# Up projections of twelve tile pairs a layer as Strassen block products, interleaved with the down projection of the chunk before

## The reference, cut to what matters

```python
for l in range(2):
    mod = (silu(c) @ w_ada[l] + b_ada[l])[:, None, :]          # 6 x 1024
    sh1, sc1, g1, sh2, sc2, g2 = jnp.split(mod, 6, axis=-1)
    ...                                                         # mixers
    x = x + g1 * (concat(y_conv, y_ret) @ w_out[l])
    h2 = rms_norm(x, norm2_g[l]) * (1.0 + sc2) + sh2
    x = x + g2 * (jnp.square(jax.nn.relu(h2 @ w_up[l])) @ w_down[l])
return rms_norm(x, final_g)
```

## Time and profile before

| | |
|---|---|
| median of 3 runs | 1188.54 us (1188.49 to 1188.67) |
| the profiled execution | 1189.33 us |
| its span, first to last instruction | 1187.5 us |
| mean granted TensorE clock | 0.989 of full |
| w_raw loads | 200 of 512 KB, median 3.3 us to landing |
| ada loads | 80 of 512 KB, median 4.7 us to landing |

### The profile page before, as it was taken

The page is one execution under the profiler, slowest core; times in us unless marked ns, Lnnn a source line. Parts: engine busy times, 40 slices in busy tenths (PEclk is TensorE's granted clock), DMA queues, the critical chain, the costliest instruction groups (busy, mean ns, idle before and its releaser), DMA issues.

```text
span 1187.5 us, 17267 instructions
## 1 busy us (share of the span) xinstructions
PE 1154.9 (97%) x5690; PEld 974.5 (82%) x5690; DVE 656.8 (55%) x870; ACT 440.6 (37%) x623; POOL 252.4 (21%) x193
## 2 busy tenths in 40 slices
PE   4999999999999999999999999999999999999996
PEld 2787888998888888888997788889988888888886
DVE  6877887577434435443268778776754323333333
ACT  6644444245331224322244544434533122343220
POOL 4385010313110012111115801013211000122110
PEclk7999999999999999999999999999999999999998
DMA  9774334335433533532146433423443222323212
GB/s 349 293 283 142 124 106 142 107 108 177 159 124 112 187 126 122 180 104 93 67 143 242 150 118 117 152 97 102 156 165 119 94 101 88 107 88 106 88 36 73
DMA packets 46910, 161.75 MB, mean 136 GB/s; under 512 B 5520, under 2 KB 7696, under 8 KB 46736
## 3 DMA queue, kind: packets, MB, share of 16 engines
q1 hardware_dynamic: 46864, 161.13, 39.2%
HBM read 159.01 MB, written 2.10 MB: 136 GB/s over the span
## 4 chain that ended last, share of the span: by engine, by line
PE 91%; DVE 3%; issue 2%; ACT 1%; DMA 1%; SPq 0%; POOL 0%; DVEq 0%; ACTq 0%; POOLq 0%
PE ps L322 28%; PE ps L324 28%; PE ps L323 28%; PE ps L498 1%; PE ps L483 1%; DMA w_raw<-weights 1%; PE ps L362 1%; PE ps L364 1%; PE ps L363 1%; DVE w_lo L795 1%; ACT w_hi L584 1%; DVE h_lo L871 0%; DVE ada_raw L806 0%; ACT h_hi L605 0%; PE ps L354 0%
## 5 line engine op out<-in xcount | busy, mean ns | idle before, releaser
L795 DVE TENSOR_TENSOR w_lo<-w_raw,w_hi 128x1024 fp32r<-128x1024 f32 x193 | 253.1, 1314 | 320.0 <-ACT w_hi L584 317.8
L322 PE MATMUL ps<-h_hi,w_hi 128*128 128x512 f32 (+1 forms) x960 | 363.2, 378 | 3.4 <-issue 1.8
L324 PE MATMUL ps<-h_hi,w_lo 128*128 128x512 f32 (+1 forms) x960 | 360.2, 375 | 0.0
L323 PE MATMUL ps<-h_lo,w_hi 128*128 128x512 f32 (+1 forms) x960 | 360.0, 375 | 0.0
L584 ACT CAST w_hi<-w_raw 128x1024 fp32r<-128x1024 f32 x196 | 204.6, 1046 | 243.9 <-PE ps L324 230.9
L322 PE MATMUL ps<-u_hi,w_hi 128*128 128x512 f32 (+1 forms) x576 | 211.0, 366 | 0.0
L322 PEld LDWEIGHTS ps<-h_hi,w_hi 128*128 128x128 f32 x960 | 180.7, 188 | 36.8 <-issue 2.0
L323 PE MATMUL ps<-u_lo,w_hi 128*128 128x512 f32 (+1 forms) x576 | 210.5, 365 | 0.0
L324 PE MATMUL ps<-u_hi,w_lo 128*128 128x512 f32 (+1 forms) x576 | 210.5, 365 | 0.0
L324 PEld LDWEIGHTS ps<-h_hi,w_lo 128*128 128x128 f32 x960 | 180.7, 188 | 32.9
L323 PEld LDWEIGHTS ps<-h_lo,w_hi 128*128 128x128 f32 x960 | 180.8, 188 | 32.2
(11 more groups left out here) (126 smaller groups left out, 1048.7 us busy)
## 6 DMA issues: line engine op xcount, KB each, us to landing
w_raw<-weights SPq DMA_DIRECT2D x200, 512.0 KB, 3.3
ada_raw<-ada SPq DMA_DIRECT2D x80, 512.0 KB, 4.7
arena<-ada SPq DMA_DIRECT2D x16, 512.0 KB, 15.2
x<-xT SPq DMA_DIRECT2D x2, 1024.0 KB, 6.7
outT<-x SPq DMA_DIRECT2D x8, 256.0 KB, 2.3
tab<-tables SPq DMA_DIRECT2D x1, 1024.0 KB, 17.1
tab<-tables SPq DMA_DIRECT2D x1, 512.0 KB, 14.6
ident<-identity SPq DMA_DIRECT2D x1, 64.0 KB, 2.0
```

The source lines that it names most:

```text
L322: nc.tensor.matmul(out, wh, hi, start=first, stop=False, skip_group_check=True)
L323: nc.tensor.matmul(out, wh, lo, start=False, stop=False, skip_group_check=True)
L324: return nc.tensor.matmul(out, wl, hi, start=False, stop=last, skip_group_check=True)
L795: nc.vector.tensor_tensor(w_lo[:, j, :], w_raw[:, j, :], w_hi[:, j, :].bitcast(F32), ALU.subtract).then_inc(w_lo_done, 1)
```

## The change

The MLP now goes in 8 chunks of 4 up tiles (`CHUNK = 4`). Chunk 0 is `first_step`, chunk 1 four plain up units; the other 24 tiles are 12 pairs. In the stream, each step of four units from unit 40 on has two up units (slots 0, 1) and two down units (slots 2, 3), which hold the weights of four output tiles for the chunk before. `down` adds four k blocks a tile, so each output tile is updated by a residual 8 times a layer rather than 2 times. The last chunk's down goes in token halves for all eight tiles (`down_half`).

A pair of up tiles is a 2 x 2 block product (weight blocks: two tiles by two halves of the width; input blocks: two halves of the width by two token halves of 256), computed in the Winograd form of Strassen's scheme: seven products of 4 k blocks, with S1 to S4 sums of raw weight blocks (VectorE, per pair) and T1 to T4 differences of the input blocks (VectorE, once a layer), each split in high and low part. ScalarE copies partial results between PSUM banks, VectorE adds two.

```diff
-                    ...                                       # up and down loops of 4 units, twice
+            def pair(u, l, p, evac):
+                def product(bank, w_high, w_low, high, low, first=False):
+                    out = ps[:, bank, HALVES[0]]
+                    for k in range(4):
+                        ...                                   # three matmuls of 256 columns
+                pe.wait_ge(evac_act, evac)
+                pe.wait_ge(c2_added, l * (2 * PAIRS) + p * 2 + 4)
+                pe.wait_ge(w_lo_done, u + (SLOTS + 1))
+                raw(C11, 0, 0, 0, 0, first=True).then_inc(pair_ps, 1)
+                pe.wait_ge(t_split, l * 4 + 4)
+                pe.wait_ge(s_split, l * (4 * PAIRS) + p * 4 + 1)
+                mixed(M7, s_hi[:, S3, :], s_lo[:, S3, :], T3, first=True).then_inc(pair_ps, 1)
+                pe.wait_ge(s_split, l * (4 * PAIRS) + p * 4 + 3)
+                pe.wait_ge(pair_copied, l * (4 * PAIRS) + p * 4 + 1)
+                mixed(C12, s_hi[:, S2, :], s_lo[:, S2, :], T2).then_inc(pair_ps, 1)
+                raw(C11, 0, 1, 4, 0).then_inc(pair_ps, 1)
+                pe.wait_ge(pair_copied, l * (4 * PAIRS) + p * 4 + 3)
+                mixed(C12, s_hi[:, S1, :], s_lo[:, S1, :], T1).then_inc(pair_ps, 1)
+                pe.wait_ge(w_lo_done, u + (SLOTS + 2))
+                mixed(C21, w_hi[:, 1, T:2 * T], w_lo[:, 1, T:2 * T], T4).then_inc(pair_ps, 1)
+                pe.wait_ge(s_split, l * (4 * PAIRS) + p * 4 + 4)
+                pe.wait_ge(pair_copied, l * (4 * PAIRS) + p * 4 + 4)
+                product(C12, s_hi[:, S4, :], s_lo[:, S4, :], ...).then_inc(pe_unit, 2)
...
+                first_step(u0 + U_UP, xs + XS_H2, n, added + SQ_MIX)
+                for i in range(2):
+                    for j in range(2):
+                        pe.wait_ge(evac_act, ea + (EA_UP + 2 * i + j + 1))
+                        unit(u0 + (U_PLAIN + 4 * i + j), j, 2 * i + j, h_hi, h_lo)
+                    down(u0 + (U_PLAIN + 4 * i), xs + (XS_U + CHUNK), ed + (2 + ED_DOWN + 4 * i), 0)
+                with pe.Fori(0, 3) as i:
+                    for q in range(4):
+                        pair(...)
+                        down(...)
```

```diff
-                load_step(l, 8, 0, 0)
-                with sp.Fori(0, 4) as i:
-                    load_step(l, i + 9, 2, b0 + i * 2 + 24, since=2)
...
+                load_step(l, 8, 4, b0 + 24)
+                load_step(l, 9, 4, b0 + 28)
+                load_step(l, 10, 0, 0)
                 with sp.Fori(0, 3) as i:
+                    for q in range(4):
+                        load_step(l, i * 4 + (11 + q), 0, 0)
+                        if q % 2 == 0:
+                            with sp.If(l < DEPTH - 1):
+                                for a in range(2):
+                                    load_ada(b0 + i * 4 + (32 + q + a), a, 2)
+                load_step(l, 23, 0, 0)
+                with sp.If(l < DEPTH - 1):
+                    for a in range(4):
+                        load_ada(b0 + (44 + a), a % 2, 2)
...                                                          # VectorE, output projection
                     residual(j, j, M_GATE1)
                     split_lo(l, 7, j)
+                    if j:
+                        gate_ada(j - 1)
...
                     residual(SLOTS + j, OUT_BANK[0][j], M_GATE1, HALVES[0])
+                    if j == 0:
+                        gate_ada(3)
```

VectorE's order in one period of the pair loop (pair p, with the preparation of pair p + 1 in it), and its end:

```diff
+                        residuals(i * 16 + (U_PAIR - 4 + 4 * q), 1 - q % 2)
+                        split_lo(l, step, 3)
+                        if q % 2 == 0: ...                    # layer 0: gate_pair, two ada tiles
+                        next_early()                          # pair_has(2): S3; pair_has(5): S1, S2
+                        pair_has(6)
+                        ...                                   # two adds of 256 columns from PSUM
+                        next_late()                           # after the pair's last product: S4
+                        next_low()                            # low parts of S3, S1, S2
+                        split_lo(l, step + 1, 0)
+                        u_low(2 * q, i * 8 + 8, 2 * q)
+                        split_lo(l, step + 1, 1, slice(T, D) if q < 3 else slice(0, D))
+                        u_low(2 * q + 1, i * 8 + 8, 2 * q + 1)
+                        s_low(p + 1, S4, 4)
+                        split_lo(l, step + 1, 2)
...
+                with dve.If(l < DEPTH - 1):
+                    gate_pair(22, 12)
+                    gate_pair(23, 14)
+                    ...                                       # norm_gain
+                residuals(U_LAST - 4, 1)
+                split_lo(l, 23, 3)
+                for m in range(KT):
+                    ...                                       # half residuals; then between or final
```

```diff
-                for s in range(6, SQ_MLP):
-                    if s == 8:
+                for s in range(SQ_MLP):
+                    if s == 12:
                         with pool.If(l < DEPTH - 1):
                             ...                               # split_lo(l, 24, 1)
```

More of the change, by code:

```diff
@@ new lines, in down_half @@
+            def down_half(j, half, evac):
+                for m in (2 * j, 2 * j + 1):
+                    bank = LAST_BANK[half][m]
+                    if half == 0 and m >= 4:
+                        pe.wait_ge(evac_dve, evac + (0 if m < 6 else m - 5))
+                    if half:
+                        pe.wait_ge(evac_dve, evac + (m + 3 if m < 4 else m + 5))
+                    for k in range(CHUNK):
+                        mm = three(bank, j, CHUNK * (m % 2) + k, u_hi[:, CHUNK + k, :], u_lo[:, CHUNK + k, :],
+                                   k == 0, k == CHUNK - 1, HALVES[half])
+                    if half and m % 2:
+                        mm.then_inc(pe_unit, 1)
+                    else:
+                        mm.then_inc(pe_half, 1)
@@ L533, in _ @@
                             spread(n, 0, HALVES[0])
-                for half in range(2):
[L536 to L552, removed]
@@ new lines, in _ @@
+                n, added = l * 2 + 2, l * SQ + SQ_MIX
+                pe.wait_ge(evac_act, ea + EA)
+                pe.wait_ge(c2_added, l * (2 * PAIRS) + (2 * PAIRS + 4))
+                pe.wait_ge(xs_lo, xs + (XS_U + 32))
+                for half in range(2):
+                    for j in range(SLOTS):
+                        if half == 0:
+                            pe.wait_ge(w_lo_done, u0 + (U_LAST + j + SLOTS + 1))
+                        down_half(j, half, ed + (2 + ED_LAST))
+                        if half and j == 0:
+                            mean_squares(n, 0, added + KT)
+                        if half and j == 1:
+                            spread(n, 0, HALVES[0])
@@ L748, in _ @@
                 between(l, 8, l * 2 + 1, 1, lambda j: out_square(1, j))
[L749 to L763, removed]
@@ L765, in _ @@
-                added = l * SQ + SQ_MIX
[L766 to L770, removed]
-                        nc.scalar.activation(buf_a[:, m, :], x[:, bass.ds(i * 2 + m, 1), :].rearrange("p a t -> p (a t)"),
-                                             ACT.Square).then_inc(sq_ready, 1)
-                        split_hi(l, i + 21, 2 * m + 1)
@@ new lines, in t_second @@
+                def t_second():
+                    for t, of, half, seen in ((T2, T1, 1, 2), (T4, T2, 0, 4)):
+                        dve.wait_ge(t_raw, l * 5 + seen)
+                        for k in range(4):
+                            mm = nc.vector.scalar_tensor_tensor(out=t_of(t, k), in0=xr_all[:, 4 + k, HALVES[half]],
+                                                                scalar=mod[:, M_SH2 + 4 + k:M_SH2 + 5 + k],
+                                                                in1=t_of(of, k), op0=ALU.add, op1=ALU.subtract)
+                        mm.then_inc(t_raw, 1)
@@ new lines, in residuals, with gate_pair @@
+                def residuals(u, group):
+                    for m in range(4):
+                        if m % 2 == 0:
+                            pe_has(l, u + (2 + m // 2))
+                        residual(4 * group + m, 4 + m, M_GATE2)
+                def gate_pair(pair_at, col):
+                    for j in range(2):
+                        ada_pair(l, pair_at, col, j, later=True)
+                t_first()
+                split_lo(l, 9, 0)
+                split_lo(l, 9, 1)
+                u_low(0, 0, 0)
@@ new lines, in _ @@
+                split_lo(l, 10, 2)
+                split_lo(l, 10, 3)
+                residuals(U_PLAIN, 0)
+                raw_loaded(11)
+                s3_sum()
+                s1_sum()
+                s2_sum(0)
+                s4_sum(0)
+                split_lo(l, 11, 0)
+                u_low(6, 0, 6)
+                t_low(T1, 3)
+                split_lo(l, 11, 1, slice(T, D))
+                u_low(7, 0, 7)
+                t_low(T4, 4)
```

(16 more changed lines are left out.)

415 lines of the change are left out of this document (290 added, 125 removed).

## The result

The changed kernel takes 1195.76 us (median; 1194.33 to 1196.70), the kernel before, beside it, 1188.61. The ratio is 1.0056, 95% interval 1.0044 to 1.0068: 7 us **slower**, where 1185.5 had been forecast. The profiled execution took 1195.69 with a span of 1193.8, against 1189.33 and 1187.5. The sum of the prediction, -3.0 us, is held against this +6.3 (of the spans).

The account below looks back on a forecast made before the run. TensorE, busy 97% of the span, was taken as the bound. Terms of -19.2, +10.7, +2.0, +2.0 and +1.5 sum to -3.0 us on 1189.33, giving 1186.3, or 1185.5 as median; range 1177 to 1194.

Parts of the forecast that it names:

- matmuls of the pairs: Up-tile pairs: 84 matmuls of 256 columns replace 48 of 512, gaining 0.80 us a pair, 24 pairs: -19.2 us.
- pair loop, starved or refetched: Pair loop: other engines keep up with TensorE and no wait is added, costed at 0.
- output projection, waits, both layers: Moved ada pairs, loaded behind weights, delay the mean of squares by 5.35 us a layer: +10.7 us.
- its clock: Output projection: the gap drops TensorE to 1.2 GHz in one layer of two: +2.0 us (0 to 4.5).
- end of layer 0, wait for x: Last two ada pairs stand in front of the last full down's residuals, so TensorE waits: +2.0 us (0 to 4).
- the clock there: End of layer 0: no clock loss was counted behind the wait for x, 0.
- layer boundary: More residuals behind the spread, and GpSimd's weight split behind four tiles' adds: +1.5 us (0.5 to 4).
- start, heads, tail: Rest of the kernel: no change in time was counted, 0.
- (a): Pair loop: TensorE refetches its code at four inner back edges, 7.4 us, giving 1192.9; chance 0.16.
- (c): Pair loop starves: a wait of 0.5 us in each of 24 periods, 12 us, giving 1197.5; chance 0.10.
- rival (d): Output projections: the clock falls in both layers and stays down through the half, +2.5 us, giving 1188.0; chance 0.10.

Follow-up runs that it names:

- E1: Changed kernel with the loads of ada 24 to 27 issued ahead of step 8's weight loads: 1184.10 us.
- E3: Changed kernel with both edits, ada 24 to 27 loaded ahead of step 8's weights and last residuals ahead of the last ada pair: 1180.62 us.
- E7: E6 with GpSimd's split for the next layer's first weights put before its 9th add of a square, not its 13th: 1173.49 us.
- E6: E3 with VectorE's reductions of ada 26 and 27 put behind the half residuals and the norm's gain: 1174.07 us, ratio 0.9871 to the kernel before.
- E8: E3 with VectorE reducing ada 24, 25 and 26 in front of the split of the same slot, not behind it: 1177.95 us.
- E4: Changed kernel with 24 unused matmuls of 256 columns filling part of the gap ahead of the mean of squares, both layers: 1192.50 us.
- E2: Changed kernel with the last four residuals and slot 3's split moved ahead of the last ada pair at the end of layer 0: 1192.51 us.

## Why the prediction was wrong

Its steps, with what the two profiled executions show (us):

```
step                                          forecast   measured
matmuls of the pairs                             -19.2      -18.7
pair loop, starved or refetched                    0          0
output projection, waits, both layers            +10.7      +14.4
its clock                                         +2.0       +3.8
end of layer 0, wait for x                        +2.0       +3.0
the clock there                                    0         +1.5
layer boundary                                    +1.5       +3.2
start, heads, tail                                 0         -0.9
```

A wait is counted here as what is missing between two matmul starts beyond their pace; the list of waits above shows 0.1 to 0.2 us less for each.

**The step that failed** is the price of the moved ada pairs in the output projections, the largest cost of the sum: 12.7 us had been put there (10.7 for the waits, 2.0 for the clock), and 18.2 were measured. The mechanism, loads queued behind weights that wait for VectorE, was right. Its walk took a load to be ready sooner and a reduction to be shorter than they were here, and the clock fell in both layers, not in one.

- **Matmuls**: right to 0.5. 2 x 9.35. Half-width matmuls at 120.0 ns and eight products turned to seven give what the earlier trace rows give. The spacing of 109 ns, estimated from "TensorE: Matmul & The Clock Gate", section Back-to-back issue gap, of the Trainium skill, did not appear; that section gives its formula for an isolated matmul, not for a stream of them.
- **Rivals (a) and (c)**: out. The list of waits has one "issue" entry of 1.7 us, at the outer back edge, as in the earlier trace rows, and none at the pair loop's. VectorE's and ScalarE's slack was enough.
- **Output projection, waits**: 1.09 + 1.39 + 5.10 = 7.6 us are missing between matmuls in layer 0 (two splits, then ssum) and 1.18 + 1.39 + 4.24 = 6.8 in layer 1; 5.35 each was forecast. The mechanism was the one named (in E1 9.9 us of these two stages go with the order of the loads alone). Two things had been mis-sized. The landing was taken as 4.25 for all four, and the last took 5.2 until its reduction, though the earlier trace rows had a median of 4.7. And the reduction was priced at 1.15 to 1.22 from places where GpSimd was idle; in layer 0 one took 2.31 and one 1.56. The two errors give about one microsecond each there: the last load went out at 234.33 where the walk had 233.4, and the mean of squares came at 244.63 where it had 242.6. The trace of before held the warning: the split at 221.72 took 1.65 beside an add of squares, and two reductions a layer in the up tiles, which the prediction did not look at, took 2.06 beside GpSimd's squares. VectorE, before:

```profile
270.97 2.06 DVE L806 CUSTOM_DVE_ANT_0 ada_raw<-ada_raw,c_act 128x1024 f32<-128x1024 f32 x1
```

- **Its clock**: forecast as one fall in two layers at 2.0. It fell in both, and the matmuls behind it took 2.0 and 1.7 us more than those of the kernel before. That is rival (d), which had a chance of 0.10 (+2.5 on the sum; measured +1.8). The forecast counted on a fall only behind a gap of 4.1 us; E1 and E3 show falls at 1.9.
- **End of layer 0**: the wait for x was 3.0 for 2.0, since both last loads were awaited (1.90 and 1.75 us of VectorE's idle time). The clock's fall behind it had been put at nothing, without a reason. Sum of what its matmuls took over their pace: 1.5.
- **Layer boundary**: twice the forecast. The stage is 7.7 us longer; less 3.0 for the wait for x and 1.5 for the clock that leaves 3.2: 1.4 before GpSimd's split, 1.3 before low parts, and small ones.

All errors but the last have one sign: +0.5, +3.7, +1.8, +1.0, +1.5, +1.7. The range's upper end, 1194, did not cover several terms being late together, though they have a common cause: the clock fell only behind waits, so each term that adds a wait can add a fall.

**What remains open**: why the clock fell behind some gaps and not behind others of equal length (below), and which wait at the layer boundary would be last if E7's were gone.

## What to carry to other kernels

Saving matmuls pays only if the work that is pushed out of the way finds idle time elsewhere: here 18.7 us of shorter products were real, and displaced side work (four ada tiles a layer, issued behind weights that wait for VectorE itself) cost 18.2, and the new order at the end of the layer 7.7. Look at where displaced loads stand in an in-order queue, and at what stands behind their consumer; then move them by need: the same change with three such edits (E6) is 1.3% faster than the kernel before instead of 0.6% slower. A gap on TensorE is to be priced with the clock behind it.

## What the runs showed of the hardware

- **VectorE beside GpSimd.** The reduction of 128 x 1024 with both inputs in SBUF took 1.21 to 1.23 us alone and up to 2.32 when it started inside a 128 x 512 add of GpSimd (E3, E6, the changed kernel): it ended 1.08 us behind the add, however early it had begun. The subtraction that makes a low part did the same (2.30 in E8, 1.65 in the kernel before). Reductions whose second input is in PSUM (59 to 100 us, beside the q and k tiles) took 1.20 to 1.22 though they began inside GpSimd's operations of 1.3 to 2.3 us.
- **The clock.** It fell behind gaps between matmuls of 5.1, 4.2 and 3.0 us (changed kernel), 2.0 in layer 0 of E4, 1.9 in both layers of E1, in layer 1 of E3 and at the outer back edge in E2. It did not behind 1.8 in layer 1 of E4, 1.9 in layer 0 of E3, 2.0 at the outer back edge of the kernel before, 2.6 at the end of layer 0 in E1 and 3.2 there in E4. Each fall cost 1.5 to 2.0 us beyond the gap (what the matmuls behind it took over their pace: 1.6 in both layers of E1, 1.5 in E3, 2.0 in layer 0 of the changed kernel). What decides between gaps of equal length is not shown. Executions of one kernel seem to differ in it: of 21 of the kernel before, whose traced one has no fall before its tail, the nine with a mean granted clock of 0.998 took 1188.0 to 1188.7 us and the three with 0.995 took 1190.6 to 1190.8. Only one of each kernel was traced, so this is a hint.
